# Conditioning vector as row products on VectorE instead of column sums with a TensorE reduction, and a fourth product bank

## The reference, cut to what matters

```
cs = jax.nn.silu(c)                                          # c: (1, 1024)
shift, scale, gate = jnp.split(cs @ mod_w[layer] + mod_b[layer], 3, axis=-1)   # mod_w: (2, 1024, 3072)
shift, scale = jnp.split(cs @ kv_mod_w + kv_mod_b, 2, axis=-1)                 # kv_mod_w: (1024, 2048)
h = _modulate(_rmsnorm(x, norm_g), shift, scale)             # h * (1 + scale) + shift
x = x + gate * mixer(h)
```

## Time and profile before

| | us |
|---|---|
| median of 3 runs (839.86 to 842.18) | 840.02 |
| the profiled execution, its own time | 839.71 |
| its span, first to last instruction | 837.9 |
| PE busy | 793.6 (95%) |
| DVE busy | 617.8 (74%) |
| ACT busy | 402.3 (48%) |
| POOL busy | 140.4 (17%) |
| DMA, share of 16 engines | 56.9% |

### The profile page before, as it was taken

How to read it: one execution, slowest core, us unless ns; L and a number is a source line. 1 busy time by engine, 2 the same in 40 slices (tenths; PEclk the granted TensorE clock), 3 DMA queues, 4 the chain that set the end, 5 groups by cost and what they waited for, 6 DMA issues and landing times.

```text
span 837.9 us, 12941 instructions
## 1 busy us (share of the span) xinstructions
PE 793.6 (95%) x5300; PEld 726.2 (87%) x5300; DVE 617.8 (74%) x957; ACT 402.3 (48%) x484; POOL 140.4 (17%) x90
## 2 busy tenths in 40 slices
PE   6999999999999999999999999999599988999986
PEld 6999899999999898768999999998499868999964
DVE  6785898877876886766988777866579876757633
ACT  5344235454443325552444443442568866655531
POOL 0110010304433110000202244422300004000000
PEclk9999999999999999999999999999699999999998
DMA  7976449887677624434489877673235462754101
GB/s 282 353 274 221 151 163 332 300 338 276 253 255 295 233 76 139 151 119 183 154 299 324 329 296 255 258 251 121 75 105 198 157 245 101 251 201 152 51 26 50
DMA packets 25978, 173.70 MB, mean 207 GB/s; under 512 B 2880, under 2 KB 3264, under 8 KB 6592
## 3 DMA queue, kind: packets, MB, share of 16 engines
q1 hardware_dynamic: 25920, 172.89, 56.9%
HBM read 171.83 MB, written 1.05 MB: 206 GB/s over the span
## 4 chain that ended last, share of the span: by engine, by line
PE 84%; DVE 7%; ACT 4%; DMA 3%; issue 1%; DVEq 0%; POOLq 0%; ACTq 0%; SPq 0%; POOL 0%
PE bank L492 11%; PE bank L494 10%; PE bank L493 10%; PE Y L573 10%; PE Y L576 10%; PE Y L574 10%; DMA raw<-weights 2%; DVE w_low L1272 2%; PE bank L836 2%; PE bank L838 2%; PE bank L837 2%; PE Y L599 1%; PE bank L520 1%; PE bank L518 1%; PE bank L519 1%; PE mbank L608 1%
## 5 line engine op out<-in xcount | busy, mean ns | idle before, releaser
L1272 DVE TENSOR_TENSOR w_low<-raw,w_high 128x2048 fp32r<-128x2048 f32 (+2 forms) x129 | 285.0, 2226 | 53.4 <-ACT w_high L936 52.9
L936 ACT CAST w_high<-raw 128x2048 fp32r<-128x2048 f32 (+2 forms) x129 | 238.3, 1859 | 95.8 <-DMA raw<-weights 79.9
L492 PE MATMUL bank<-xT_h,w_high 128*128 128x256 f32 x736 | 211.9, 288 | 2.9 <-DVE w_low L1270 2.9
L493 PE MATMUL bank<-xT_l,w_high 128*128 128x256 f32 x736 | 209.4, 284 | 0.0
L494 PE MATMUL bank<-xT_h,w_low 128*128 128x256 f32 x736 | 209.3, 284 | 0.0
L492 PEld LDWEIGHTS bank<-xT_h,w_high 128*128 128x128 f32 x736 | 142.2, 193 | 3.3 <-DVE w_low L1270 3.3
L493 PEld LDWEIGHTS bank<-xT_l,w_high 128*128 128x128 f32 x736 | 142.3, 193 | 0.0
L494 PEld LDWEIGHTS bank<-xT_h,w_low 128*128 128x128 f32 x736 | 142.2, 193 | 0.0
L573 PE MATMUL Y<-w_high,hT_h 128*128 128x512 f32 x328 | 130.1, 397 | 5.1 <-DVE hT_l L1303 2.9
L574 PE MATMUL Y<-w_low,hT_h 128*128 128x512 f32 x328 | 128.6, 392 | 0.0
L576 PE MATMUL Y<-w_high,hT_l 128*128 128x512 f32 x328 | 102.5, 394 | 0.0
(11 more groups left out here) (224 smaller groups left out, 1394.6 us busy)
## 6 DMA issues: line engine op xcount, KB each, us to landing
raw<-weights SPq DMA_DIRECT2D x151, 1024.0 KB, 5.1
rows<-rows_in SPq DMA_DIRECT2D x9, 512.0 KB, 6.5
raw<-weights SPq DMA_DIRECT2D x4, 768.0 KB, 4.6
raw<-weights SPq DMA_DIRECT2D x4, 512.0 KB, 3.5
raw<-weights SPq DMA_DIRECT2D x2, 896.0 KB, 5.2
x<-x_in SPq DMA_DIRECT2D x2, 512.0 KB, 4.1
out<-x SPq DMA_DIRECT2D x4, 256.0 KB, 2.0
consts<-consts_in SPq DMA_DIRECT2D x1, 320.0 KB, 5.2
```

The costliest lines, as they stand in the source:

```text
L492: mm(dst, high, xh[:, kt, :], start=kt == 0, stop=False)
L493: mm(dst, high, xl[:, kt, :], start=False, stop=False)
L936: nc.scalar.copy(w_high[:, n % RING, start:COLS[n]], raw[:, s % RAW, start:COLS[n]]).then_inc(w_high_ready, 1)
L1272: tt(w_low[:, n % RING, start:COLS[n]], slot[:, start:COLS[n]], f32(w_high[:, n % RING, start:COLS[n]]), ALU.subtract).then_inc(raw_done, 1)
```

## The change

The modulation pieces now lie *row-major*: partition p holds the 1024 weights that belong to one result, for two results (2 x 1024 fp32, the same 1 MB). `c` is broadcast to all partitions as a row of 1024 (`c_row`, in the half of `kT` that is free), its silu is taken there, and one DVE instruction per result column multiplies the weights by `c_row` and sums along the row into its column of `modcol` (`accum_out`). The product itself is written back over the weights. POOL's additions, the `mod_sums` matmuls and `read_mod` fall away; the bias is added once for all 64 columns. `kT` is overwritten by the keys of the first attention, so `c_row` is loaded and its silu taken twice: at the start and behind that attention. The softplus chain moves from the start to that second place. The PSUM bank `mbank` becomes a fourth `bank`.

```diff
-PBANKS = 3
+PBANKS = 4
...
-        macc = sb("macc", [P, 2, SEQ])
...
+        c_row, c_half = kT_f[:, 1024:], area_f[:, 1024:]
...
-        mbank = ctx.enter_context(nc.psum_tensor("mbank", [P, 512], F32))
...
+                if s == 1:
+                    sp.dma_start(c_row, rows_in[9, :].partition_broadcast(P)).then_inc(c_in, 16)
...
                     if which == 2:
                         sp.wait_ge(S["scores"], nth("scores", "mla", TB * HEADS - 1))
+                        sp.dma_start(c_row, rows_in[9, :].partition_broadcast(P)).then_inc(c_in, 16)
...
-            def mod_sums(m):
-
-                pe.wait_ge(mod_added, m + 1)
-                if m:
-                    pe.wait_ge(mod_read, m)
-                for i in range(2):
-                    last = mm(mbank[:, i:i + 1], mod_acc(m)[:, 0, i * P:(i + 1) * P], ones[:, 0:1], start=True, stop=True)
-                last.then_inc(mod_summed, 1)
...
-                    mod_sums(m0 + g - 2)
                     up(PI[phase, "up", g], (phase, g))
-                tail(phase, m=m0 + FFG - 2, early=early)
+                tail(phase, early=early)
...
-            add_accumulators(range(SCMODS, SCMODS + FFG - 1))
...
-            add_accumulators(range(SCMODS + FFG - 1, NMOD))
...
-            nc.scalar.activation(cth[:, :], colrange("c"), ACT.Tanh, scale=0.5).then_inc(c_tanh, 1)
+            def tanh_of_c(n):
+                act.wait_ge(c_in, 16 * n)
+                nc.scalar.activation(c_half, c_row, ACT.Tanh, scale=0.5).then_inc(c_tanh, 1)
+
+            tanh_of_c(1)
...
+            act.wait_ge(lam_exp_in, 1)
+            nc.scalar.activation(prm[:, 7, :], prm[:, 6, :], ACT.Exp, scale=-1.0).then_inc(lam_exp, 1)
+            tanh_of_c(2)
             split_ahead(("mla", "down", MXG - 1), FILL)
...
-                        for kt in range(KT):
-                            acc, part = accumulators[:, kt % 2, :], slot[:, kt * SEQ:(kt + 1) * SEQ]
...
+                        for t in range(2):
+                            part = slot[:, t * D:(t + 1) * D]
+                            last = stt(out=part, in0=part, scalar=0.5, in1=c_row, op0=ALU.mult, op1=ALU.mult,
+                                       accum_out=modcol[:, 2 * n + t:2 * n + t + 1])
+                        last.then_inc(raw_done, 1)
...
-            def read_mod(m):
-
-                dve.wait_ge(mod_summed, m + 1)
-                tt(modcol[:, 2 * m:2 * m + 2], mbank[:, 0:2], colrange("mod_b", 2, 2 * m), ALU.add).then_inc(mod_read, 1)
...
+                tt(modcol[:, :], modcol[:, :], colrange("mod_b", 2 * NMOD), ALU.add).then_inc(mod_ready, 1)
+                dve.wait_ge(mod_ready, 1)
...
+            def silu_of_c(n):
+                dve.wait_ge(c_tanh, n)
+                link(stt(out=c_row, in0=c_half, scalar=1.0, in1=c_row, op0=ALU.add, op1=ALU.mult))
...
+            split_ahead(("mla", "down", MXG - 1), 2)
+            silu_of_c(2)
+            softplus_of_lambda()
             layer_norms("ln2", "mla", 2, FILL, FILL)
...
-            a = k_major(mod[:, n * 2 * P:(n + 1) * 2 * P], KT)
+            a = mod[:, n * 2 * P:(n + 1) * 2 * P].T.reshape(2, P, D).transpose(1, 0, 2).reshape(P, -1)
```

More of the change, by code:

```diff
@@ L577, in down, with tail @@
                 last.then_inc(summed, 1)
-            def tail(phase, th=hT_h, tl=hT_l, early=None, m=None):
+            def tail(phase, th=hT_h, tl=hT_l, early=None):
                 for b in range(TB):
@@ L586, in tail @@
                         down(phase, g, b, th, tl)
-                    if m is not None and b == 0:
-                        mod_sums(m)
             def transposes(name, src, signal=None, blocks=range(TB), z_name=None):
@@ L701, in _ @@
                         down("sc", g - 1, b)
-            tail("sc", early=lambda: transposes("ln0", x, "x_ready", [0]), m=SCMODS - 1)
-            feed_forward("ff0", SCMODS, "ln0", lambda: transposes("ln1", x, "x_ready", [0]))
+            tail("sc", early=lambda: transposes("ln0", x, "x_ready", [0]))
+            feed_forward("ff0", "ln0", lambda: transposes("ln1", x, "x_ready", [0]))
             def latent_kv(b):
@@ L760, in _ @@
                         pe.wait_ge(kpe_ready, b + 1)
-                        last = nc.tensor.transpose(dst[:, tok(b)], macc[:, b, P:2 * P], ident)
+                        last = nc.tensor.transpose(dst[:, tok(b)], area[:, 5 + b, P:2 * P], ident)
                     in_order("mla", "kpe")
@@ L882, in root @@
                     .then_inc(S["rstd_ready"], 1)
-            def add_accumulators(pieces):
-                for m in pieces:
-                    pool.wait_ge(raw_done, AT["mod", m] + 1)
-                    acc = mod_acc(m)
-                    nc.gpsimd.tensor_tensor(acc[:, 0, :], acc[:, 0, :], acc[:, 1, :], ALU.add).then_inc(mod_added, 1)
             def diagonals(layer):
@@ L1384, in modulation_parameters, with layer_norms @@
                 dve.wait_ge(prm_ready, 1)
-            def layer_norms(name, phase, before, between, after, m=None, lows=True):
+            def layer_norms(name, phase, before, between, after, lows=True):
                 last_piece = (phase, "down", GROUPS[phase] - 1)
@@ L1391, in layer_norms @@
                 layer_norm_apply(name, 0)
-                if m is not None:
-                    read_mod(m)
-                if m == NMOD - 1:
+                if name == "ln3":
                     modulation_parameters()
@@ L1465, in _, with softplus_of_lambda @@
             split_ahead(("sc", "C", 0), 0)
+            def silu_of_c(n):
+                dve.wait_ge(c_tanh, n)
+                link(stt(out=c_row, in0=c_half, scalar=1.0, in1=c_row, op0=ALU.add, op1=ALU.mult))
+            def softplus_of_lambda():
+                lam, r2, s, d, poly, s2 = colrange("lam"), prm[:, 8, :], prm[:, 9, :], prm[:, 10, :], prm[:, 11, :], prm[:, 5, :]
+                ts(HBA, colrange("rg_ba"), 0.5, None, ALU.mult)
+                link(ts(HBX, colrange("rg_bx"), 0.5, None, ALU.mult))
+                dve.wait_ge(lam_exp, 1)
+                e = prm[:, 7, :]
+                link(ts(d, e, 2.0, None, ALU.add))
+                link(nc.vector.reciprocal(d, d))
+                link(tt(s, e, d, ALU.mult))
+                link(tt(s2, s, s, ALU.mult))
+                link(ts(poly, s2, 1.0 / 15, None, ALU.mult))
+                for odd in (13, 11, 9, 7, 5, 3):
+                    link(stt(out=poly, in0=poly, scalar=1.0 / odd, in1=s2, op0=ALU.add, op1=ALU.mult))
+                link(stt(out=poly, in0=poly, scalar=1.0, in1=s, op0=ALU.add, op1=ALU.mult))
+                link(ts(r2, r2, -2.0 * RG_C / 4, None, ALU.mult))
+                link(stt(out=C4, in0=poly, scalar=-RG_C, in1=r2, op0=ALU.mult, op1=ALU.add))
             dve.wait_ge(cols_in_done, 16)
-            lam, r2, s, d, poly, s2 = colrange("lam"), prm[:, 8, :], prm[:, 9, :], prm[:, 10, :], prm[:, 11, :], prm[:, 5, :]
+            silu_of_c(1)
+            lam, r2 = colrange("lam"), prm[:, 8, :]
             link(ts(r2, lam, -1.0, 0.0, ALU.mult, ALU.max))
```

80 lines of the change are left out of this document (17 added, 63 removed).

## The result

The kernel after takes 834.1 us in the median of 4 runs (833.2 to 834.87). The kernel before took 839.94 us in 4 runs. The ratio is 0.9909, with a 95% interval from 0.9886 to 0.9932. The profiled execution took 834.45 us with a span of 832.2, where the sum of the prediction said 824.4.

What follows compares the result with a forecast made beforehand. PE's own instructions were taken to set the time in 31 of 32 places. 839.71 - 14.2 + 0.2 - 1.3 = 824.4 us, 824.7 as a median; the range 821.8 to 828.3 held a little over 8 in 10.

Steps and rivals of the forecast that it cites:

- One-column matmuls, 14.2 us: Removing PE's one-column sum matmuls at 32 places saves 0.44 us each, 14.2 us in all, between 11.5 and 16.0.
- The row products at 1.25 us, covered: DVE's multiply-and-sum takes 1.25 us, 2.5 us per piece against 2.9 before, and costs nothing on the path.
- Rival 2: DVE's row products take 2.5 us each, so PE loses 0 to 2 us: about 826 us; 8%.
- rival 4: Slower: DVE decides in the feed-forwards from 3.5 us per row product; at 3.6 us the time is 847 us; 2%.
- ln2, ln3 and the start at nothing or nearly so: Behind the first attention and at the start 0; at ln3, in the second feed-forward's tail, 0.2 us lost.
- the 0.9 us of room in the prediction: At ln2 DVE's residual sum is 1.6 us late, leaving 0.9 us before PE transposes x; cost taken as nothing.
- The fourth bank, 1.3 us: In the attentions a fourth bank shortens PE's waits for gate readouts, 1.3 us gained, bounds 0 and 3.0.
- a group of the feed-forward of 11.25 us: PE's time per feed-forward group falls from 11.69 to 11.25 us, 0.44 less, with matmul steps fixed.
- The clock term: Around ln3 and between first-attention scores and values, the lower clock may shift: 1.8 us either way, taken as 0.
- Rival 1: DVE late at ln2, behind the first attention, or half a clock stretch more: 826.5 to 828.5 us; 17%.

Runs made afterwards that it cites:

- before_nosums: The kernel before without the one-column matmuls and the PE waits in front of them (modulation not computed): 829.67 us, ratio 0.9859.
- align: The kernel after plus an unused 32-byte pad behind `cols`, putting hT and the other moved tiles back on multiples of 64 bytes: 827.11 us, ratio 0.9839.
- third: `align` with a third row product on DVE at each of the 32 places: 826.47 us.
- banks3: The kernel after with three product banks instead of four: 832.82 us, ratio 0.9896.
- align3: `align` with three product banks instead of four: 828.24 us, ratio 0.9824.
- h_off: The kernel after with three pads, so that of the moved tiles only hT_h and hT_l stay 32 bytes off a multiple of 64: 831.99 us, ratio 0.9867.
- h_on: The kernel after with pads ahead of hT_h and `kT`, so that only hT_h and hT_l are back on multiples of 64 bytes: 827.17 us, ratio 0.983.
- pad64: The kernel after with a 64-byte pad where `align` has 32, tiles still 32 bytes off a multiple of 64: 832.97 us, ratio 0.9886.
- off16: `align` with a 16-byte pad instead of 32; all built addresses equal those of `align`, so the same program on another chip: 825.95 us.
- all_off: `align` with 32 bytes more ahead of `raw`, so that every tile is 32 bytes off a multiple of 64: 828.28 us, ratio 0.9842.
- w_off: `align` with pads of 32 bytes ahead of `w_high` and 96 ahead of `x`, so w_high and w_low are 32 bytes off: 832.44 us, ratio 0.9875.
- xT192: `align` with pads of 192 bytes ahead of xT_h and 64 ahead of `stage`, so xT stands at distance 192 from w_high: 819.27 us, ratio 0.9711.
- before192: The kernel before with pads of 192 bytes ahead of xT_h and 64 ahead of `stage`: 832.49 us, ratio 0.9889.

## Why the prediction was wrong

- **"One-column matmuls, 14.2 us": right.** `before_nosums` gave 0.44 us per group (32 x 0.44 is 14.1; the sum has 14.2). `align` against the kernel before stood 13.9 us ahead by 552 us, with 31 of the 32 places behind it (31 x 0.445 = 13.8). The closeness is in part luck: 0.65 us of the lead came in the first 20 us, and 0.9 us of it was lost to a longer stretch at the lower clock at 361.
- **The row products at 1.25 us, covered: right.** 1.22 us each, and `third` had room for one more. Rival 2 (sums at half rate) and rival 4 did not occur; 1219 ns is far from the 3.5 us from which rival 4 would decide.
- **ln2, ln3 and the start at nothing or nearly so: right in what they cost.** No wait came at ln2, but DVE was 2.8 us late there and not 1.6, so it was closer than the 0.9 us of room in the prediction. The first matmul starts 0.2 us later than before.
- **The fourth bank, 1.3 us: mechanism right, size too large.** The readout waits of the earlier trace rows are gone, and the wait for ACT's copy is some 0.5 us where I had put 0.4; that is 0.25 us gained, three times, so some 0.75 us. In the first attention the 0.3 us did not come: the two waits of 0.33 us went over from L1579 to ACT's copy. In totals it doesn't show (`banks3` -1.3 us, `align3` +1.1).
- **The step that failed** is "a group of the feed-forward of 11.25 us", worked out as 11.69 - 0.44 with "PE sets the time by its own instructions" and fixed steps of 0.12 and 0.23 us. I took the steps for constants of the shapes. They hang on how far apart the two operands lie, and the change moved hT by 2080 bytes, from distance 192 to 160; a group took 11.34 us. The list of edits in the part on the change has nothing on `macc` and `cols` as space. 984 `down` matmuls at 0.0035 to 0.004 us (0.09 us of a group over 24) and 576 of 128x256 at 0.004 make 5.7 to 6.2 us (an estimate from the steps). Measured as differences of medians, `h_off` less `h_on` is 4.8, `pad64` less `align` 5.9, the kernel after less `align` 7.0; as differences of ratios, taken of 840 us, they are 3.1, 3.9 and 5.9.
- **The rest**, 827.1 against 824.7, is 2.4 us and inside the range. 0.5 is the bank's; the remainder is of the size by which one program's runs differ (825.63 to 830.93), and in `align` three short stretches at the lower clock that `off16` hasn't. The clock term, "1.8 us either way", was too narrow for that. Against the starts of `align`, the stretch at 328 us cost the kernel after 3.0 us, of which 1.1 came back at once. In the two profiled executions this makes the account of the 7.9 us between the kernel after and `align`: some 6 from the steps, 2 from this stretch.
- None of my rivals was this one. Rival 1 had the right sign and a clock stretch in it, but at its place, ln2, PE did not wait.

What stays open: why the distance matters and why with this period; what sets the pace where both occur. The Trainium skill (TensorE: Matmul & The Clock Gate, section on the step by step phases of a matmul) says that the array has two independent read ports, and that loading the next weights doesn't steal read bandwidth from the running matmul. No run shows a load that slows a matmul by itself, but the rows show an influence of the two places on each other: with equal instructions and no waits, the step stayed at 0.229 us when all tiles moved together (`all_off`) and went to 0.232 us when the weights' tiles moved against hT (`w_off`). A clash of the two streams would fit, and isn't shown.

## What to carry to other kernels

A change that frees or adds space in SBUF moves every tile behind it. This kernel, which TensorE bounds, lost 0.4 to 0.7% by that alone and gained about 1% in `xT192`. Keep the addresses fixed while you measure an edit (a pad in the place of what was removed), and compare the step between equal matmuls before looking for waits. Then try the layout on purpose: here two pads of 256 bytes in all were worth another 7.8 us in the median (827.11 to 819.27, on two chips; the ratios, 0.9839 and 0.9711, say some 11), where the change with its tiles kept in place was worth 13.8 (840.93 to 827.11).

## What the runs showed that I had not expected

- The step of float32 matmuls with a weight load each: 0.113 to 0.120 us for 128x256 and 0.227 to 0.235 us for 128x512 at the full clock, by the distance of the operands modulo 256 bytes.
- Two paces at one distance, each held for nearly every group of 72 matmuls to its end (`before192`, 11.40 and 11.69 us).
- The same program met the lower clock, for some 3 to 7 us at a time, at other places in another execution (`align` and `off16`). One such stretch cost the kernel after 3.0 us, so a single trace can't lay it to an edit.
- A VectorE product with a sum over 1024 float32 elements costs 1219 ns, no more than a subtraction of that size without one, and 80 ns of accumulator read behind it that overlap the next.
